# Attention in a hybrid gMLP / MLA decoder layer: probabilities as the stationary operand, next head's q, k, v between key steps

## The chip, the cores and the metric

One Trainium2 chip, all 8 cores. Each core computes one of the 8 sequences of the batch on its own; no data passes between cores. The metric is the device time in microseconds (us) of the slowest core.

TensorE is called PE in the profile (PEld is its weight load), VectorE DVE, ScalarE ACT, GpSimd POOL, SyncE SP. A matmul takes a stationary operand (at most 128x128, loaded into the array first) and a moving operand (up to 512 columns) and writes to a bank of PSUM. There are eight banks, each 128 partitions by 512 float32.

## The reference, cut to what matters

One decoder layer: a token-mixing sub-layer with two branches (gMLP spatial gating, and latent attention), then a gated MLP with a causal depthwise convolution. The change touches attention alone:

```python
q = (rmsnorm(q_lat, q_norm_g) @ w_uq).reshape(B, S, 16, 128 + 64)
kv = (rmsnorm(kv_lat, kv_norm_g) @ w_ukv).reshape(B, S, 16, 128 + 128)
q_nope, q_pe = q[..., :128], q[..., 128:]
k_nope, v = kv[..., :128], kv[..., 128:]
q_pe = apply_rope(q_pe, cos, sin)          # per head
k_pe = apply_rope(k_pe, cos, sin)          # one, shared by all heads
s = (q_nope @ k_nope^T + q_pe @ k_pe^T) * 192 ** -0.5      # S = 2048, causal
p = softmax(s, axis=-1)
o = p @ v                                  # (B, S, 16 heads * 128)
```

The output o of all heads goes through `w_branch_b`, is gated and added to the other branch.

## The kernel before, in words

The program of a core is written as a list of operations per engine. A helper (`P.op`, `P.dma`) notes what each operation reads and writes and puts waits on semaphores in front of it, by itself. Each engine runs its list in order. PSUM banks are tracked whole, and two engines that read one bank are kept apart. Most operations go through small helpers, so their line in the profile is that of the helper: `mm` (L338, a chain of matmuls), `act` (L345), `tt` (L349, tensor_tensor), `copy` (L363, CAST in the profile), `recip` (L366), a weight load (L217), `ada` (L400), transposes (L436).

The 2048 positions are worked in two blocks of 1024 (`blk` 0 and 1). A block goes through: norm and transpose of x, the gMLP projections and mixing, `branch` "a", `latents` (compressed q and kv, the rotary key), `attention`, `branch` "b", `wout_phase`, `ffn_up`, `ffn_down`. Queries of block 1 attend to keys of both blocks, so that block has more key steps.

Weights come through `WPool` in three slots, in a planned order, by casting DMAs issued on POOL. `next()` takes the next entry of the plan and issues loads up to `len(slots) - live` entries ahead, the current one counted. A load waits until the last readers of its slot, as far as they are written down at that point, are done. Attention uses one `pair` entry of 768 KB for two heads. In block 0, four `ada` entries of 2 MB (a part of the conditioning projection, 64 matmuls with one moving column) stand among them.

`attention` (L668) runs over 8 pairs of heads. For a pair it first computes, from `qgT` (512 x 1024) and `kvgT` (256 x 2048), all of q, k and v:

- for each half of 512 queries (`t`): the plain q of both heads (4 matmuls each, evicted by a DVE copy, L692), then the two rotary products of both heads together (4 + 4 matmuls), two DVE multiplies with cos and sin, and two DVE additions of 64 partitions each (L695 to L701). The other 64 partitions of each `Qr` are zero.
- for each head and each 512 keys: k by 2 matmuls and a DVE copy (L702 to L706).
- for each 256 keys: v of both heads by 4 matmuls of 256 columns (L713) and one ACT copy for each head (L718).

All these take their banks from `pbank`, which goes round seven of the eight, 1 to 7. Then come the two heads of the pair, one after the other (L719). For each `t` it goes over key blocks of 128 (`kb`), up to the diagonal. A step is: scores with keys stationary and queries moving (L749 plain, L750 rotary, and on the diagonal L752, which adds a mask), so that a tile holds 128 keys by up to 512 queries; the exponential by ACT into one of four `ptile`; and, two steps later, two matmuls with the exponentials moving: L759 with V stationary, which gives the output transposed (128 channels by 512 queries), and L760 with a matrix of ones stationary, which gives the sum of the exponentials in every partition. On diagonal steps the columns shrink from 512 to 384, 256, 128. At the end of a `t`, `finalize` takes the reciprocal of 128x512 and multiplies (L726, L727) into `oT`. The score banks rotate over 5 to 7; the outputs and sums stand in banks 2 and 3, or 1 and 4. At the end of each head the two pending steps are emitted before anything of the next head.

A head in block 0 has 4 + 8 = 12 steps, in block 1 12 + 16 = 28.

Of the kernel before, what the change touches and what calls it, by code (L numbers as in the profile page):

```python
# [234 lines left out]
def build():  # L235
# [34 lines left out]
    xtr = sb("xtr", [128, 10240], BF16)  # L270
# [22 lines left out]
    Qr = [scr[:, 2048:3072], scr[:, 3072:4096]]  # L293
    ptile = [scr[:, 8192 + 512 * k:8192 + 512 * (k + 1)] for k in range(4)]
    rec = scr[:, 10240:11264].bitcast(F32)
    rt1 = scr[:, 11264:12288].bitcast(F32)
    qgT = xtr[:, 0:4096].rearrange("p (c t) -> p c t", c=4)
    cos2 = xtr[:, 4096:5120]
    sin_s = xtr[:, 5120:6144]
    KV = ((scr[:, 4096:6144], scr[:, 6144:8192].rearrange("p (k d) -> p k d", k=16)),  # L300
          (xtr[:, 6144:8192], xtr[:, 8192:10240].rearrange("p (k d) -> p k d", k=16)))
# [27 lines left out]
    def pbank():  # L329
        b = 1 + prot["n"] % 7  # L330
        prot["n"] += 1
        return ps[b][:, :]
# [335 lines left out]
    def attention(plan, blk):  # L668
        T0 = blk * NT
        nk512 = (T0 + NT) // 512  # L670
        for pr in range(8):
            if plan:
                wp.declare(("pair", blk, pr), w_pair_d[pr].rearrange("p (k o) -> p k o", k=1), 1, 3072)
                if blk == 0 and pr % 2 == 1:
                    ada(True, 16 + pr // 2)
                continue
            rot["lo"], rot["cnt"] = 5, 3
            if pr == 0:
                P.op("pool", lambda e: e.memset(Qr[0][64:128, :], 0.0), writes=[Qr[0]])
                P.op("pool", lambda e: e.memset(Qr[1][0:64, :], 0.0), writes=[Qr[1]])  # L680
            w = wp.next(("pair", blk, pr))[:, 0, :]
            qn = w[:, 0:1024].rearrange("p (k o) -> p k o", k=4)
            qr = w[:, 1024:1536].rearrange("p (k o) -> p k o", k=4)
            qs = w[:, 1536:2048].rearrange("p (k o) -> p k o", k=4)
            kn = w[:, 2048:2560].rearrange("p (k o) -> p k o", k=2)
            vv = w[:, 2560:3072].rearrange("p (k o) -> p k o", k=2)
            for t in range(2):
                tsl = slice(t * 512, (t + 1) * 512)
                q = qgT[:, :, tsl]
                for hd in range(2):  # L690
                    out = pbank()
                    mm(out, [(qn[:, c, hd * 128:(hd + 1) * 128], q[:, c, :]) for c in range(4)], [qn, q])  # L692
                    copy(QnT[hd][:, tsl], out)
                pr_, psw = pbank(), pbank()
                for out, wsel in ((pr_, qr), (psw, qs)):  # L695
                    mm(out, [(wsel[:, c, :], q[:, c, :]) for c in range(4)], [wsel, q])
                tt(rt1, pr_, cos2[:, tsl], ALU.mult)
                tt(rec, psw, sin_s[:, tsl], ALU.mult)
                for hd in range(2):
                    p0 = 64 * hd  # L700
                    tt(Qr[hd][p0:p0 + 64, tsl], rt1[p0:p0 + 64, :], rec[p0:p0 + 64, :], ALU.add)  # L701
            for hd in range(2):  # L702
                for kt in range(nk512):
                    out, kv = pbank(), kvgT[:, :, kt * 512:(kt + 1) * 512]
                    mm(out, [(kn[:, c, hd * 128:(hd + 1) * 128], kv[:, c, :]) for c in range(2)], [kn, kv])
                    copy(KV[hd][0][:, kt * 512:(kt + 1) * 512], out)  # L706
            for kb0 in range(0, 4 * nk512, 2):
                out, kv = pbank(), kvgT[:, :, kb0 * 128:(kb0 + 2) * 128]

                def mmv(e, out=out, kv=kv, vv=vv):  # L710
                    for i in range(2):
# [4 lines left out]
                P.op("pe", mmv, reads=[vv, kv], writes=[out])  # L716
                for hd in range(2):
                    act(KV[hd][1][:, kb0:kb0 + 2, :], out.rearrange("p (i h d) -> p i h d", i=2, h=2)[:, :, hd, :], AF.Copy)  # L718
            for hd in range(2):  # L719
                h = 2 * pr + hd  # L720
                Kh, Vh = KV[hd]
                pend = []
                cnt = 0

                def finalize(t, po, psm):
                    recip(rec, psm)  # L726
                    tt(oT[:, h, t * 512:(t + 1) * 512], po, rec, ALU.mult)  # L727

                def emit_pend(ent):
                    f, rds, po, psm, fin = ent  # L730
                    P.op("pe", f, reads=rds, writes=[po, psm])
                    if fin is not None:
                        finalize(fin, po, psm)

                for t in range(2):
                    qa = (T0 + 512 * t) // 128
                    nkb = qa + 4
                    po, psm = (ps[2][:, :], ps[3][:, :]) if t == 0 else (ps[1][:, :], ps[4][:, :])
                    for kb in range(nkb):
                        i = kb - qa  # L740
                        c0 = 128 * i if i > 0 else 0
                        qsl = slice(t * 512 + c0, (t + 1) * 512)
                        out = gbank()
                        pt = ptile[cnt % 4][:, c0:512]
                        cnt += 1
                        ks = slice(kb * 128, (kb + 1) * 128)

                        def mms(e, out=out, i=i, c0=c0, qsl=qsl, ks=ks, hd=hd, Kh=Kh):
                            e.matmul(out[:, c0:512], lhsT=Kh[:, ks], rhs=QnT[hd][:, qsl], start=True, stop=False)  # L749
                            ins = e.matmul(out[:, c0:512], lhsT=kpe_dup[:, ks], rhs=Qr[hd][:, qsl], start=False, stop=(i < 0))  # L750
                            if i >= 0:
                                ins = e.matmul(out[:, c0:c0 + 128], lhsT=ident[:, :], rhs=maskneg[:, :], start=False, stop=True)  # L752
                            return ins
                        P.op("pe", mms, reads=[Kh[:, ks], kpe_dup[:, ks], QnT[hd][:, qsl], Qr[hd][:, qsl], ident[:, :], maskneg[:, :]],
                             writes=[out])
                        act(pt, out[:, c0:512], AF.Exp, scale=SCALE)

                        def mmo(e, kb=kb, c0=c0, pt=pt, nkb=nkb, po=po, psm=psm, Vh=Vh):
                            e.matmul(po[:, c0:512], lhsT=Vh[:, kb, :], rhs=pt, start=(kb == 0), stop=(kb == nkb - 1))  # L759
                            return e.matmul(psm[:, c0:512], lhsT=ones[:, :], rhs=pt, start=(kb == 0), stop=(kb == nkb - 1))  # L760
                        pend.append((mmo, [Vh[:, kb, :], pt, ones[:, :]], po, psm, t if kb == nkb - 1 else None))
                        if len(pend) > 2:
                            emit_pend(pend.pop(0))
                for ent in pend:
                    emit_pend(ent)
            if blk == 0 and pr % 2 == 1:
                ada(False, 16 + pr // 2)
            rot["lo"], rot["cnt"] = 4, 4

    def sumsq(bank, c):  # L770
        act(bank, bank, AF.Square, accum_out=stat[:, c:c + 1])
# [236 lines left out]
```

How the kernel before makes its waits and increments, by code:

```python
        def run(e, lst):  # L167
            for waits, fn, inc in lst:
                for s, v in waits:
                    e.wait_ge(semobj[s], v)
                if fn is None:
                    continue
                ins = fn(e)
                if inc is not None:
                    ins.then_inc(semobj[inc[0]], inc[1])
```

## Time and profile before

| | us |
|---|---|
| median of 3 runs | 5176.35 |
| lowest, highest | 4950.4, 5376.13 |
| the profiled execution, its own time | 4950.76 |
| its span, first to last instruction, slowest core (core 4) | 4949.0 |
| spans of the 8 cores | 4927.9 to 4949.0 |
| PE busy, mean granted clock on core 4 | 4377.7 (88%), 0.957 |

The span is what the rows are read from; the profiled execution's own time is 1.8 us longer. "Busy" counts a matmul from its start to the end of its passage through the array. Matmuls overlap in this, so the rate of a stream is read from the distance between starts and not from the duration. A granted clock of 1 is 2.4 GHz, a half is 1.2 GHz.

### The profile page before, as it was taken

To read this page: it belongs to the slowest core of one execution; us is meant where nothing else is said; L and a number is where in the kernel's file an instruction comes from. 1 tells how busy PE (TensorE), PEld (TensorE's weight loads), DVE (VectorE), ACT (ScalarE), POOL (GpSimd) and SP (SyncE) were. 2 spreads that over 40 slices of the span, in tenths; PEclk is the share of its full clock that TensorE was granted. 3 is DMA by queue.
4 is the path that set the end of the run, shared out by engine and by line. 5 is a ranking of instruction groups with operands and counts; after the bars stand their busy time and mean duration, and the time that the engine had idled before them with its cause. 6 is when DMAs were issued, how large, how long until landed. Compare 5 with 4: busy or idle time off the path is not lost.

```text
span 4949.0 us, 59571 instructions; the slowest of 8 cores (4927.9 to 4949.0 us)
## 1 busy us (share of the span) xinstructions
PE 4377.7 (88%) x22392; PEld 2056.5 (42%) x22392; DVE 1743.0 (35%) x2672; ACT 1476.6 (30%) x2775; POOL 200.9 (4%) x197
## 2 busy tenths in 40 slices
PE   0579998899979999999287999999999899999994
PEld 0334444444434444444143444444444344444442
DVE  0222007752155555400314114443422455555002
ACT  0331013420154444300133103555501444444000
POOL 1000000000000000000000000000000000000000
PEclk9989999999989999999688999999999999999997
DMA  9738872357874545445652542001234555453544
GB/s 153 134 52 109 107 119 43 54 93 104 116 178 72 82 70 84 64 73 87 194 108 42 84 69 43 14 7 24 45 73 79 149 94 86 69 85 58 83 74 148
DMA packets 330441, 423.56 MB, mean 86 GB/s; under 512 B 8496, under 2 KB 315696, under 8 KB 319408
## 3 DMA queue, kind: packets, MB, share of 16 engines
q0 software_dynamic: 312352, 328.22, 43.8%
q1 hardware_dynamic: 17808, 91.54, 5.6%
q8 instruction: 183, 3.00, 0.3%
q14 instruction: 98, 0.80, 0.1%
HBM read 714.37 MB, written 33.57 MB: 151 GB/s over the span
## 4 chain that ended last, share of the span: by engine, by line
PE 78%; DMA 8%; DVE 7%; ACT 3%; issue 3%; another core or an unknown queue 0%; DVEq 0%; SPq 0%; POOL 0%; ACTq 0%; POOLq 0%
PE ps L338 56%; PE ps L887 12%; PE ps L759 2%; DMA wslot<-w_ada 2%; PE ps L760 2%; DMA sb_big<-out 2%; PE ps L749 2%; PE ps L750 2%; ACT sb_scr L345 2%; DVE sb_scr L366 2%; DMA wslot<-w_ag 1%; DVE sb_scr L359 1%; DMA wslot<-w_out 1%; DMA wslot<-w_in 1%; DVE sb_big L359 1%
## 5 line engine op out<-in xcount | busy, mean ns | idle before, releaser
L345 ACT ACTIVATE sb_scr<-ps 128x512 f32<-128x512 f32 (+4 forms) x1304 | 709.4, 551 | 2145.2 <-PE ps L338 1534.2
L338 PE MATMUL ps<-sb_big,wslot 128*128 128x512 bf16 x5632 | 1239.3, 383 | 25.6 <-DMA wslot<-w_ag 9.2
L338 PE MATMUL ps<-sb_mrg,wslot 128*128 128x512 bf16 x5632 | 1219.0, 380 | 0.0
L338 PEld LDWEIGHTS ps<-sb_big,wslot 128*128 128x128 bf16 x5632 | 554.1, 99 | 700.8 <-issue 52.4
L338 PEld LDWEIGHTS ps<-sb_mrg,wslot 128*128 128x128 bf16 x5632 | 551.9, 98 | 666.3 <-issue 4.0
L359 DVE SCALAR_TENSOR_TENSOR sb_scr<-sb_scr,sb_cols 128x512 f32<-128x512 f32 x704 | 528.8, 751 | 541.7 <-ACT sb_scr L345 505.1
L887 PE MATMUL ps<-wslot,sb_big 128*128 128x512 bf16 x2048 | 452.5, 379 | 0.0
L366 DVE RECIPROCAL sb_scr<-ps 128x512 f32<-128x512 f32 x64 | 214.9, 3357 | 322.4 <-PE ps L760 321.5
L345 ACT ACTIVATE ps<-ps 128x512 f32<-128x512 f32 x128 | 74.5, 582 | 809.9 <-DVE sb_big L349 387.8
L349 DVE TENSOR_TENSOR sb_mrg<-ps,sb_scr 128x512 bf16<-128x512 f32 (+1 forms) x96 | 66.4, 691 | 689.2 <-PE ps L338 413.7
L887 PEld LDWEIGHTS ps<-wslot,sb_big 128*128 128x128 bf16 x2048 | 200.4, 98 | 241.6
L345 ACT ACTIVATE sb_scr<-ps,sb_cols 128x512 f32<-128x512 f32 x352 | 271.8, 772 | 0.0
L338 PE MATMUL ps<-wslot,sb_mrg 128*128 128x512 bf16 x1024 | 237.2, 395 | 5.7 <-DMA wslot<-w_out 5.7
L349 DVE TENSOR_TENSOR sb_scr<-ps,sb_scr 128x512 f32<-128x512 f32 x80 | 55.3, 691 | 498.1 <-PE ps L338 357.3
L338 PE MATMUL ps<-wslot,sb_big 128*128 128x512 bf16 x1024 | 223.7, 382 | 0.0
L436 PE MATMUL ps<-sb_ident,sb_scr 128*128 128x128 bf16 x512 | 52.2, 283 | 193.7 <-DVE sb_scr L354 92.8
L750 PE MATMUL ps<-sb_scr,sb_kpe_dup 128*128 128x512 bf16 (+3 forms) x640 | 222.7, 348 | 0.0
L760 PE MATMUL ps<-sb_scr,sb_ones 128*128 128x512 bf16 (+3 forms) x640 | 220.6, 347 | 0.0
L345 ACT ACTIVATE sb_scr<-sb_scr 128x512 bf16<-128x512 f32 (+1 forms) x208 | 171.8, 826 | 74.2 <-DVE sb_scr L359 46.3
L338 PE MATMUL ps<-sb_xtr,wslot 128*128 128x512 bf16 x512 | 130.8, 416 | 38.7 <-DVE sb_big L349 20.7
L400 PE MATMUL ps<-sb_scb,wslot 128*128 128x1 bf16 x1536 | 42.6, 164 | 133.5 <-DMA wslot<-w_ada 133.5
L338 PEld LDWEIGHTS ps<-wslot,sb_mrg 128*128 128x128 bf16 x1024 | 103.3, 102 | 133.9 <-issue 24.5
(112 smaller groups left out, 2973.5 us busy)
## 6 DMA issues: line engine op xcount, KB each, us to landing
wslot<-w_up POOLq DMA_DIRECT2D x44, 2048.0 KB, 14.7
wslot<-w_ada POOLq DMA_DIRECT2D x24, 2048.0 KB, 28.3
wslot<-w_down POOLq DMA_DIRECT2D x32, 1408.0 KB, 10.7
sb_scr<-x SPq DMA_DIRECT2D x32, 1024.0 KB, 6.4
wslot<-w_in POOLq DMA_DIRECT2D x16, 2048.0 KB, 17.1
wslot<-w_ag POOLq DMA_DIRECT2D x16, 2048.0 KB, 14.7
wslot<-w_bg POOLq DMA_DIRECT2D x16, 2048.0 KB, 14.9
wslot<-w_out POOLq DMA_DIRECT2D x8, 2048.0 KB, 15.5
```

The costliest lines, as they stand in the source:

```text
L338: ins = e.matmul(out, lhsT=a, rhs=b, start=(k == 0), stop=(k == len(pairs) - 1))
L345: P.op("act", lambda e: e.activation(out=out, in_=in_, func=func, **kw), reads=[in_] + extra + list(reads), writes=[out] + acc + list(writes))
L349: P.op(eng, lambda e: e.tensor_tensor(out=out, in0=in0, in1=in1, op=op), reads=[in0, in1], writes=[out])
L359: P.op("dve", lambda e: e.scalar_tensor_tensor(out=out, in0=in0, scalar=s, in1=in1, op0=op0, op1=op1), reads=[in0, in1] + extra, writes=[out])
L366: P.op("dve", lambda e: e.reciprocal(out=out, in_=in_), reads=[in_], writes=[out])
L400: ins = e.matmul(out[:, oc:oc + 1], lhsT=wv[:, kc, oc * 128:(oc + 1) * 128], rhs=scb[:, kc:kc + 1], start=(kc == 0), stop=(kc == KC - 1))
L436: ins = e.transpose(out=pv[:, k * 128:(k + 1) * 128], in_=src[:, kc * 128:(kc + 1) * 128], identity=ident[:, :])
L749: e.matmul(out[:, c0:512], lhsT=Kh[:, ks], rhs=QnT[hd][:, qsl], start=True, stop=False)
L750: ins = e.matmul(out[:, c0:512], lhsT=kpe_dup[:, ks], rhs=Qr[hd][:, qsl], start=False, stop=(i < 0))
L759: e.matmul(po[:, c0:512], lhsT=Vh[:, kb, :], rhs=pt, start=(kb == 0), stop=(kb == nkb - 1))
L760: return e.matmul(psm[:, c0:512], lhsT=ones[:, :], rhs=pt, start=(kb == 0), stop=(kb == nkb - 1))
L887: ins = e.matmul(out, lhsT=g[k], rhs=wv[:, k, :], start=(q == 0 and k == 0), stop=(q == 3 and k == 10))
```

## The change

Only `attention` and the tiles it uses change.

- The exponentials of a step become the stationary operand, 128 keys by 128 queries at a time, and V the moving one. V has a 129th column of ones, so that column 128 of the result is the sum. A step has one to four such matmuls of 129 columns. The output stands with queries in the partitions, four quarters in two banks. L760 is gone.
- At the end of a `t`, per bank: a reciprocal of two columns and a multiply into `on` (bf16). Three steps later four transposes (`turn_o`) bring it back to channels by queries, and a DVE copy writes `oT`.
- q, k and v are computed per head by `gen(h)`, as a list of tasks. The tasks of head h + 1 are dealt out evenly between the key steps of head h. Head 0's stand alone ahead of the loop. Rotary q is still made for two heads at once, in the list of the even head, and `Qr` is double now. The sine product is written back to its PSUM bank. v comes per head, 8 matmuls of 128 columns and one ACT copy for 512 keys.
- The pending attends go on across heads; nothing drains between them.
- Banks: 0 to 3 hold outputs, in two pairs that alternate. All else (scores, tasks, transposes, `ada`) rotates over 4 to 7.
- `wp.live` is 2 in attention, so loads are issued one entry less ahead. `ada` entries stand at other places of the plan.

The diff, cut to its core:

```diff
+    Qr = [[oT[:, 14, :], oT[:, 15, :]], [scr[:, 2048:3072], scr[:, 3072:4096]]]
+    on = scr[:, 10256:10768].rearrange("p (s d) -> p s d", s=4)
+    KV = ((scr[:, 4096:6144], scr[:, 6144:8208].rearrange("p (k d) -> p k d", k=16)),
+          (xtr[:, 6144:8192], xtr[:, 8192:10256].rearrange("p (k d) -> p k d", k=16)))
...
+                if blk == 0 and (pr in (2, 4, 6) or pr == 7):
+                    ada(True, 16 + (pr - 1) // 2)
+            return
+        for i in range(2):
+            for z in (Qr[0][i], Qr[1][i]):
+                half = z[64:128, :] if i == 0 else z[0:64, :]
+                P.op("pool", lambda e, half=half: e.memset(half, 0.0), writes=[z])
+            one = KV[i][1][:, :, 128:129]
+            P.op("pool", lambda e, one=one: e.memset(one, 1.0), writes=[one, Qr[0][0], Qr[0][1], Qr[1][0], Qr[1][1]])
...
+            def rope(t):
+                pr_, psw = gbank(), gbank()
...
+                tt(rt1, pr_, cos2[:, tsl], ALU.mult)
+                tt(psw, psw, sin_s[:, tsl], ALU.mult)
+                for i in range(2):
+                    p0 = 64 * i
+                    tt(Qr[pr % 2][i][p0:p0 + 64, tsl], rt1[p0:p0 + 64, :], psw[p0:p0 + 64, :], ALU.add)
...
+                    for i in range(4):
                         for c in range(2):
-                            ins = e.matmul(out[:, i * 256:(i + 1) * 256], lhsT=kv[:, c, i * 128:(i + 1) * 128], rhs=vv[:, c, :],
+                            ins = e.matmul(out[:, i * 128:(i + 1) * 128], lhsT=kv[:, c, i * 128:(i + 1) * 128], rhs=vv[:, c, dsl],
                                            start=(c == 0), stop=(c == 1))
...
+                act(Vh[:, 4 * kt:4 * kt + 4, 0:128], out.rearrange("p (i d) -> p i d", i=4), AF.Copy)
+
+            work = [lambda t=t: nope(t) for t in range(2)]
+            if hd == 0:
+                work += [lambda t=t: rope(t) for t in range(2)]
+            for kt in range(nk512):
+                work += [lambda kt=kt: keys(kt), lambda kt=kt: values(kt)]
+            return work
...
-                            e.matmul(po[:, c0:512], lhsT=Vh[:, kb, :], rhs=pt, start=(kb == 0), stop=(kb == nkb - 1))
-                            return e.matmul(psm[:, c0:512], lhsT=ones[:, :], rhs=pt, start=(kb == 0), stop=(kb == nkb - 1))
+        def attend(h, t, kb, nkb, pt, s0, po):
+            v = KV[h % 2][1][:, kb, :]
+            def go(e):
+                for s in range(s0, 4):
+                    ins = e.matmul(po[s // 2][:, s % 2 * 256:s % 2 * 256 + 129], lhsT=pt[:, s * 128:(s + 1) * 128], rhs=v,
+                                   start=(kb == 0 and s % 2 == 0), stop=(kb == nkb - 4 + s), skip_group_check=True)
+                return ins
+            P.op("pe", go, reads=[pt[:, s0 * 128:512], v], writes=po)
+            if kb == nkb - 1:
+                for b in range(2):
+                    o3 = po[b].rearrange("p (s c) -> p s c", s=2)
+                    rs = stat[:, 48 + 2 * b:50 + 2 * b]
+                    recip(rs.unsqueeze(2), o3[:, :, 128:129])
+                    tt(on[:, 2 * b:2 * b + 2, :], o3[:, :, 0:128], rs.unsqueeze(2).broadcast_to([128, 2, 128]), ALU.mult)
+                late.append([3, lambda: turn_o(h, t)])
...
+        wp.live = 2
+        for w in gen(0):
+            w()
+        for h in range(16):
+            nxt = gen(h + 1) if h < 15 else []
+            steps = sum((T0 + 512 * t) // 128 + 4 for t in range(2))
+            done, total = 0, len(nxt)
+            for t in range(2):
...
+                for kb in range(nkb):
+                    pt, s0 = scores(h, t, kb, qa, k)
+                    k += 1
+                    pend.append((h, t, kb, nkb, pt, s0, po))
+                    if len(pend) > 2:
+                        attend(*pend.pop(0))
+                    step()
+                    done += 1
+                    while nxt and len(nxt) > (steps - 2 - done) * total / steps:
+                        nxt.pop(0)()
...
+            if blk == 0 and h % 4 == 3:
+                ada(False, 16 + h // 4)
+        wp.live = 1
+        while pend:
+            attend(*pend.pop(0))
+        while late:
+            late.pop(0)[1]()
```

`gbank` takes the next bank of the rotation (4 to 7 outside the old `attention`). `step` counts the entries of `late` down once per key step and runs those that reach zero.

## Rows read from the trace of the kernel before

**Rows 1.** The page, engine totals and costliest groups, whole span.

```profile
PE 4377.7 (88%) x22392; PEld 2056.5 (42%) x22392; DVE 1743.0 (35%) x2672; ACT 1476.6 (30%) x2775; POOL 200.9 (4%) x197
...
L366 DVE RECIPROCAL sb_scr<-ps 128x512 f32<-128x512 f32 x64 | 214.9, 3357 | 322.4 <-PE ps L760 321.5
...
L760 PE MATMUL ps<-sb_scr,sb_ones 128*128 128x512 bf16 (+3 forms) x640 | 220.6, 347 | 0.0
```

**Rows 2.** Both attention stages: length; busy PE, PEld, DVE, ACT, POOL (instructions); clock; DMA.

```profile
791.19:1066.96 275.77, 239.66 (x1537) 124.75 (x1536) 210.47 (x195) 110.54 (x257) 10.16 (x12) 0.96 0.41 68
...
3061.22:3586.90 525.68, 490.02 (x2561) 233.37 (x2559) 229.19 (x224) 281.34 (x577) 6.64 (x9) 0.98 0.13 24
```

**Rows 3.** Timeline of PE, full steps in block 1: start, duration.

```profile
3093.70 0.38 PE L749 MATMUL ps<-sb_scr 128*128 128x512 bf16 x1
...
3098.45 0.22 PE L752 MATMUL ps<-sb_maskneg,sb_ident 128*128 128x128 bf16 x1
```

**Rows 4.** Timelines, pauses of PE at pair starts, first exponentials, stage ends.

```profile
860.38 8.74 PE L338 MATMUL ps<-sb_xtr,wslot 128*128 128x512 bf16 x28 [2.06 <-DVE sb_modc L349]
...
1070.79 9.39 PE L338 MATMUL ps<-sb_big,wslot 128*128 128x512 bf16 x36 [2.08 <-DVE sb_scr L366]
...
3080.52 0.38 PE L759 MATMUL ps<-sb_scr 128*128 128x512 bf16 x1 [0.89 <-ACT sb_scr L345]
...
3124.13 1.89 PE L338 MATMUL ps<-sb_xtr,wslot 128*128 128x512 bf16 x8
3128.75 6.93 PE L338 MATMUL ps<-sb_xtr,wslot 128*128 128x512 bf16 x24 [2.73 <-DVE sb_big L349]
...
3139.62 0.59 PE L338 MATMUL ps<-sb_kvgT,wslot 128*128 128x512 bf16 x2 [0.92 <-DVE sb_scr L363]
3140.22 4.62 PE L713 MATMUL ps<-wslot,sb_kvgT 128*128 128x256 bf16 x32
...
3590.65 9.59 PE L338 MATMUL ps<-sb_big,wslot 128*128 128x512 bf16 x31 [3.68 <-DVE sb_scr L366]
```

**Rows 5.** Timelines, short matmuls with a weight load each, and the loads.

```profile
806.04 0.22 PE L749 MATMUL ps<-sb_scr 128*128 128x128 bf16 x1
806.10 0.22 PE L750 MATMUL ps<-sb_scr,sb_kpe_dup 128*128 128x128 bf16 x1
...
806.21 0.33 PE L759 MATMUL ps<-sb_scr 128*128 128x384 bf16 x1
...
1066.96 1.74 PE L400 MATMUL ps<-sb_scb,wslot 128*128 128x1 bf16 x64
...
1392.60 1.06 PE L436 MATMUL ps<-sb_ident,sb_scr 128*128 128x128 bf16 x16
1393.49 0.81 PE L338 MATMUL ps<-wslot,sb_mrg 128*128 128x512 bf16 x3
...
L760 PEld LDWEIGHTS ps<-sb_scr,sb_ones 128*128 128x128 bf16 x192 | 18.8, 98 | 6.4
```

**Rows 6.** Groups of DVE in block 0's stage (busy us, mean ns), and a timeline row.

```profile
L366 DVE RECIPROCAL sb_scr<-ps 128x512 f32<-128x512 f32 x32 | 107.4, 3357 | 45.0 <-PE ps L760 44.2
...
L349 DVE TENSOR_TENSOR sb_scr<-sb_scr 64x512 bf16<-64x512 f32 x32 | 22.0, 687 | 2.2 <-DVE sb_scr L349 0.2
...
1071.35 0.15 DVE L349 TENSOR_TENSOR sb_modc<-ps,sb_cols 128x4 f32<-128x4 f32 x1
```

**Rows 7.** ACT: exponentials in block 1, and a stage's table loads (one each stage).

```profile
3079.78 1.57 ACT L345 ACTIVATE sb_scr<-ps 128x512 bf16<-128x512 f32 x3
...
L345 ACT ACT_TABLE_LOAD x1 | 1.3, 1283 | 0.0
```

**Rows 8.** Weight loads around block 0's attention (780 to 1200 us).

```profile
wslot<-w_ada POOLq DMA_DIRECT2D x7, 2048.0 KB, 17.3
wslot<-w_bg POOLq DMA_DIRECT2D x6, 2048.0 KB, 16.0
...
874.18 0.54 POOL L217 DMA_DIRECT2D wslot<-w_pair  x1 [15.04 <-PE ps L713]
```

More of the change, by code:

```diff
@@ L269, in build @@
     scr = sb("scr", [128, 12288], BF16)
-    xtr = sb("xtr", [128, 10240], BF16)
+    xtr = sb("xtr", [128, 10272], BF16)
     kvgT = sb("kvgT", [128, 2, S], BF16)
@@ L292, in build @@
     QnT = [scr[:, 0:1024], scr[:, 1024:2048]]
[L293 to L296, printed above, removed]
+    Qr = [[oT[:, 14, :], oT[:, 15, :]], [scr[:, 2048:3072], scr[:, 3072:4096]]]
+    ptile = [scr[:, 8208 + 512 * k:8208 + 512 * (k + 1)] for k in range(4)]
+    on = scr[:, 10256:10768].rearrange("p (s d) -> p s d", s=4)
+    rt1 = scr[:, 10768:11792].bitcast(F32)
     qgT = xtr[:, 0:4096].rearrange("p (c t) -> p c t", c=4)
@@ L670, in attention @@
         nk512 = (T0 + NT) // 512
-        for pr in range(8):
-            if plan:
+        if plan:
+            for pr in range(8):
                 wp.declare(("pair", blk, pr), w_pair_d[pr].rearrange("p (k o) -> p k o", k=1), 1, 3072)
[L674 to L687, printed above, removed]
+                if blk == 0 and (pr in (2, 4, 6) or pr == 7):
+                    ada(True, 16 + (pr - 1) // 2)
+            return
@@ new lines, in attention, with weights @@
+        for i in range(2):
[4 more added lines that the diff above has]
+            P.op("pool", lambda e, one=one: e.memset(one, 1.0), writes=[one, Qr[0][0], Qr[0][1], Qr[1][0], Qr[1][1]])
+        wcur = {}
+        def weights(pr):
+            if pr not in wcur:
+                w = wp.next(("pair", blk, pr))[:, 0, :]
+                wcur[pr] = [w[:, a:b].rearrange("p (k o) -> p k o", k=k) for a, b, k in
+                            ((0, 1024, 4), (1024, 1536, 4), (1536, 2048, 4), (2048, 2560, 2), (2560, 3072, 2))]
+            return wcur[pr]
@@ L688, in attention, with gen, nope @@
+        def gen(h):
+            pr, hd = h // 2, h % 2
+            Kh, Vh = KV[hd]
+            dsl = slice(hd * 128, (hd + 1) * 128)
+            def nope(t):
+                qn = weights(pr)[0]
+                out, q = gbank(), qgT[:, :, t * 512:(t + 1) * 512]
+                mm(out, [(qn[:, c, dsl], q[:, c, :]) for c in range(4)], [qn, q])
+                copy(QnT[hd][:, t * 512:(t + 1) * 512], out)
+            def rope(t):
                 tsl = slice(t * 512, (t + 1) * 512)
                 q = qgT[:, :, tsl]
[L690 to L693, printed above, removed]
@@ L694, in attention @@
-                pr_, psw = pbank(), pbank()
-                for out, wsel in ((pr_, qr), (psw, qs)):
-                    mm(out, [(wsel[:, c, :], q[:, c, :]) for c in range(4)], [wsel, q])
-                tt(rt1, pr_, cos2[:, tsl], ALU.mult)
[L698 to L711, printed above, removed]
+                pr_, psw = gbank(), gbank()
+                for out, w in ((pr_, weights(pr)[1]), (psw, weights(pr)[2])):
+                    mm(out, [(w[:, c, :], q[:, c, :]) for c in range(4)], [w, q])
+                tt(rt1, pr_, cos2[:, tsl], ALU.mult)
+                tt(psw, psw, sin_s[:, tsl], ALU.mult)
@@ new lines, in rope, with keys, values @@
+                for i in range(2):
+                    p0 = 64 * i
+                    tt(Qr[pr % 2][i][p0:p0 + 64, tsl], rt1[p0:p0 + 64, :], psw[p0:p0 + 64, :], ALU.add)
+            def keys(kt):
+                kn = weights(pr)[3]
+                out, kv = gbank(), kvgT[:, :, kt * 512:(kt + 1) * 512]
+                mm(out, [(kn[:, c, dsl], kv[:, c, :]) for c in range(2)], [kn, kv])
+                copy(Kh[:, kt * 512:(kt + 1) * 512], out)
+            def values(kt):
+                vv = weights(pr)[4]
+                out, kv = gbank(), kvgT[:, :, kt * 512:(kt + 1) * 512]
+                def go(e):
+                    for i in range(4):
@@ L712, in mmv @@
                         for c in range(2):
-                            ins = e.matmul(out[:, i * 256:(i + 1) * 256], lhsT=kv[:, c, i * 128:(i + 1) * 128], rhs=vv[:, c, :],
+                            ins = e.matmul(out[:, i * 128:(i + 1) * 128], lhsT=kv[:, c, i * 128:(i + 1) * 128], rhs=vv[:, c, dsl],
                                            start=(c == 0), stop=(c == 1))
                     return ins
-                P.op("pe", mmv, reads=[vv, kv], writes=[out])
-                for hd in range(2):
-                    act(KV[hd][1][:, kb0:kb0 + 2, :], out.rearrange("p (i h d) -> p i h d", i=2, h=2)[:, :, hd, :], AF.Copy)
@@ L719, in attention @@
[L719 to L758, printed above, removed]
-                            e.matmul(po[:, c0:512], lhsT=Vh[:, kb, :], rhs=pt, start=(kb == 0), stop=(kb == nkb - 1))
-                            return e.matmul(psm[:, c0:512], lhsT=ones[:, :], rhs=pt, start=(kb == 0), stop=(kb == nkb - 1))
[L761 to L765, printed above, removed]
@@ L766, in attention @@
-            if blk == 0 and pr % 2 == 1:
-                ada(False, 16 + pr // 2)
-            rot["lo"], rot["cnt"] = 4, 4
+                P.op("pe", go, reads=[vv, kv], writes=[out])
+                act(Vh[:, 4 * kt:4 * kt + 4, 0:128], out.rearrange("p (i d) -> p i d", i=4), AF.Copy)
[4 more added lines that the diff above has]
+                work += [lambda kt=kt: keys(kt), lambda kt=kt: values(kt)]
@@ new lines, in gen, with scores, go @@
+            return work
+        pend, late = [], []
+        ocnt = [0]
+        def scores(h, t, kb, qa, k):
+            hd = h % 2
+            i = kb - qa
+            c0 = 128 * i if i > 0 else 0
+            qsl = slice(t * 512 + c0, (t + 1) * 512)
+            out, pt = gbank(), ptile[k % 4]
+            ks = slice(kb * 128, (kb + 1) * 128)
+            Kh, Qh, Rh = KV[hd][0][:, ks], QnT[hd][:, qsl], Qr[h // 2 % 2][hd][:, qsl]
+            kp = kpe_dup[:, ks]
+            def go(e):
+                e.matmul(out[:, c0:512], lhsT=Kh, rhs=Qh, start=True, stop=False)
+                ins = e.matmul(out[:, c0:512], lhsT=kp, rhs=Rh, start=False, stop=(i < 0))
+                if i >= 0:
+                    ins = e.matmul(out[:, c0:c0 + 128], lhsT=ident[:, :], rhs=maskneg[:, :], start=False, stop=True)
+                return ins
+            P.op("pe", go, reads=[Kh, kp, Qh, Rh, ident[:, :], maskneg[:, :]], writes=[out])
+            act(pt[:, c0:512], out[:, c0:512], AF.Exp, scale=SCALE)
+            return pt, max(i, 0)
@@ new lines, in turn_o, with go, step @@
+        def turn_o(h, t):
+            out = gbank().bitcast(BF16)[:, 0:512]
+            def go(e):
+                for s in range(4):
+                    ins = e.transpose(out=out[:, s * 128:(s + 1) * 128], in_=on[:, s, :], identity=ident[:, :])
+                return ins
+            P.op("pe", go, reads=[on[:, :, :], ident[:, :]], writes=[out])
+            copy(oT[:, h, t * 512:(t + 1) * 512], out)
+        def step():
+            for ent in late:
+                ent[0] -= 1
+            while late and late[0][0] <= 0:
+                late.pop(0)[1]()
@@ new lines, in attention @@
+        wp.live = 2
+        for w in gen(0):
+            w()
+        k = 0
+        for h in range(16):
[3 more added lines that the diff above has]
+            for t in range(2):
+                qa = (T0 + 512 * t) // 128
+                nkb = qa + 4
+                po = [ps[2 * (ocnt[0] % 2)][:, :], ps[2 * (ocnt[0] % 2) + 1][:, :]]
+                ocnt[0] += 1
+                for kb in range(nkb):
[8 more added lines that the diff above has]
+                        nxt.pop(0)()
+            while nxt:
+                nxt.pop(0)()
+            if blk == 0 and h % 4 == 3:
+                ada(False, 16 + h // 4)
@@ L770, in sumsq @@
+        wp.live = 1
+        while pend:
+            attend(*pend.pop(0))
+        while late:
+            late.pop(0)[1]()
     def sumsq(bank, c):
```

4 lines of the change are left out of this document (2 added, 2 removed).

## The prediction

> **What bounds the kernel now.** I read four views in this order. First the engine totals of the page [rows 1]: TensorE is busy 88% of the span, DVE and ACT a third of it. So a change pays only where it takes columns or idle time from TensorE. Two groups of the page touch this change: the ones-matmul of L760 (640 of them) and the RECIPROCAL of L366, 3.36 us each.
>
> Second, the two attention stages as windows [rows 2]: 275.8 us in block 0 (first q matmul to last L760) and 525.7 us in block 1. I compare each with what its matmuls need back to back. In a run of full steps 22 matmuls of 512 columns start in 4.75 us, 215.7 ns each, that is 512 columns at 2.4 GHz plus 2.3 ns [rows 3]; I use this pair, columns/2.4 ns + 2.3 ns, for every matmul. Block 0 issues 507,904 columns in 1344 matmuls plus three `ada` calls of 1.6 us: 211.6 + 3.1 + 4.8 = 219.5 us. Block 1 issues 1,097,728 columns in 2560: 457.4 + 5.9 = 463.3 us. Left over: 56.3 and 62.4 us. To these I add the pauses after the last L760 of each stage, 2.1 and 3.7 us [rows 4]. Gaps are 124.5 us in all.
>
> Third, where these gaps are [rows 4]. At a pair's start TensorE stops 2.73 us after eight matmuls: a bank handed to the new pair's q still holds the sums of the old head, and DVE reads them for 3.36 us. There are casts to wait for at 0.92 us, the first exponentials at 0.89 us, and in block 1 the 32 value matmuls take 4.62 us where 32 of 109 ns would take 3.5: two ACT copies per bank pace them. After some pauses the clock stands at its lower level: 28 matmuls take 8.74 us behind `ada` and a 2.06 us pause, where 6.0 is normal (nearly all the excess is 15 matmuls near 0.4 us apart, the 1.2 GHz level). The same costs some 2.5 us on other pair starts.
>
> **The change, part by part.**
>
> *Ones-matmul out, probabilities stationary.* Per head and block the old kernel moved 4608 (block 0) or 12,800 (block 1) columns through L759 and as many through L760. Now every 128-query quarter is a matmul of 129 columns: 10 + 26 = 36 in block 0, 42 + 58 = 100 in block 1, or 4644 and 12,900 columns. Turning adds 8 matmuls of 128 columns a head. Q, k and score columns stay; value matmuls become twice as many at half the width. So per head block 0 now has 12,288 (q, k, v) + 10,240 (scores, mask) + 4644 + 1024 = 28,196 columns in 112 matmuls: 12.0 us; sixteen heads and three `ada`: 196.9 us. Block 1: 16,384 + 26,624 + 12,900 + 1024 = 56,932 in 236: 24.3 us; sixteen heads: 388.2 us. Against 219.5 and 463.3 this saves 22.6 + 75.1 = 97.7 us.
>
> The doubtful price is that of a short matmul with a new weight load each: 2176 of L759's successor, 256 transposes, 768 value matmuls, 3200 in all. No row shows 129 columns. Rows 5 show 128: from 806.04 three score matmuls of 128 columns with a load each, and the L759 behind them, start 0.17 us over all, 55 ns apart, and sixteen transposes start over 0.89 us, 55.6 ns each, with sixteen loads. The lower end is 53.8 ns (129 columns at 2.4 GHz), the upper 154 ns, if the 98 ns that a load shows ran in series. I take 56: the transposes are the same shape, and 64 loads go through in 1.74 us, so loads alone can come every 27 ns.
>
> The Trainium skill speaks against this part: "TensorE: Matmul & The Clock Gate", section "Back-to-back issue gap", puts a sustained stream of load and matmul pairs at about 81 ns for 128 columns. By that, as an estimate from that page, 3200 x 25 = 81 us would be lost and the time would be 4857 us. The sixteen-transpose row here disagrees, at 55.6 ns.
>
> *Normalising.* 64 reciprocals of 128x512 (3.36 us) leave DVE for reciprocals of two columns, half-width multiplies and a cast: by the 0.69 us of 128x512 and the 0.15 us of a 128x4 operation [rows 6], about 2 x (0.15 + 0.4) + 0.65 = 1.75 us a pass instead of 4.05. The new result waits three steps for its transposes, some 2 us, so TensorE should seldom wait.
>
> *Dealing out.* The gap at each pair's start goes: scores always have a next instruction, nothing drains between heads, and the output banks (0 to 3) are no longer handed to other work. Value evictions fall between exponentials. ACT then has per full step 0.5 us (three exponentials in 1.57 us with one latency of 0.6 inside [rows 7]) against 0.65 us of TensorE, plus 0.5 us per four value blocks: about 14 us of 24.3 a head in block 1, 5.5 of 12 in block 0. It stays covered. Copy and Exp alternating costs no table load: a stage has one load [rows 7], though seven later pairs go from copies to exponentials. Were it not so, about 90 insertions at 2 x 1.28 us would be some 230 us of ACT; the count excludes it.
>
> What is late next is the rope work. It takes two of four banks, shared now with scores; DVE then needs two multiplies and two additions of 0.69 us each, 2.8 us [rows 6], the second bank until the last. TensorE comes round to that bank after three others. In block 1 tasks lie about two steps apart (28 steps, 12 tasks), so 1.95 to 2.3 us pass: 0.4 us stall per rope, 1.2 a pair with neighbours, 8 us. In block 0, eight tasks go in twelve steps and both rope tasks follow each other, so about 2 us a pair, 14 us. Bounds: nothing (the DVE queue is empty), and 2.8 us for each of 32 ropes, 90 us.
>
> *Remaining gaps.* The first head's q, k, v stand alone with four banks instead of seven and are DVE-paced, 2 us, then the first exponentials cost 1.5 us: 7 us for both blocks. Other heads 0.3 us each: 9. At the end two last attends, DVE and the transposes have no cover: 2 us, twice. Lower clock behind `ada`: 5. Sum 14 + 8 + 7 + 9 + 4 + 5 = 47; it replaces 124.5, so 77.5 us go.
>
> *Queues.* POOL issues weight loads one ahead less. But a load goes as soon as the last reader of its slot is done, since POOL waits for nothing else: the `pair` load at 874.18 was released by a matmul of the pair before [rows 8]. Counting slots through the new order, the one that receives an `ada` block is free at least two heads (24 us) ahead of its use, against 17.3 us to landing [rows 8]; the first `w_bg` block of 16.0 us likewise. Cost zero; without that cover, up to 16 us for each of four. The four half-tile memsets and the ones columns are some 4 us on idle POOL ahead of the first rope: hidden behind the last latents.
>
> **Sum.** 97.7 + 77.5 = 175 us. The profiled execution took 4950.8 us (span 4949.0 plus 1.8). 4950.8 - 175 = **4776 us**. The median of the runs shown is 5176.4; the profiled run agrees with the lowest of them (4950.4), and I forecast from there.
>
> **Rivals.**
>
> A. *Loads exposed at each instruction boundary.* Weights are now fresh from ACT, and a load can't go ahead of the semaphore that releases it. 640 steps x 98 ns = 63 us: 4839. For: the stationary operand is new in each step, where V and ones were old. Against: at 806.21 an L759, which has a wait in front of it in the program, starts on the 55 ns beat [rows 5]. The Trainium skill's 81 ns named above would be the same trouble spread over all short matmuls, at 4857 us; no chance is set aside for it beyond this rival's.
>
> B. *Bank waits replace the drains.* Four banks serve scores, q, k, v, ropes and transposes. 288 dealt tasks at 0.3 us, half of the 0.60 to 0.92 us cast waits of today: 86 us, of which 22 us are in my sum, plus slow clock behind some: with ropes at their upper bound 4850 to 4900, middle 4862. For: DVE has 210 of 276 us in block 0 now [rows 2]. Against: the reciprocals alone are 107 us of that [rows 6].
>
> C. *Loads in series (slower).* Place: the four matmuls of each attend. Price: 98 ns for each of 3200 short matmuls, 314 us: 5090. It decides as soon as a short matmul costs 55 ns more than its columns (3200 x 55 = 175), a spacing of 111 ns. Against: both chains of rows 5.
>
> D. *Nearly no gaps:* floor 585 us plus 7: about 4735.
>
> **How the numbers follow.** Forecast (4740 to 4815) 0.68; A 0.10; B 0.12; C 0.04; D 0.06. Leaving out C and the upper half of B, the range is 4735 to 4850. A measurement of this kernel tells about 2% from no change, a boundary of 4852 us. Faster: 0.68 + 0.10 + 0.06 + a quarter of B = 0.87. Within 2%: the rest of B, 0.09. Slower: C, 0.04.
>
> **What would show it.** Right: L759's successor starts about 56 ns apart in runs of four; the stages take about 225 and 408 us; RECIPROCAL has only small forms in attention; no pause of TensorE over 2 us at pair boundaries; DVE below 75% in block 0; weight loads cause no wait. Wrong: spacing above 80 ns (A or C), or many TensorE waits on DVE and ACT with banks as their cause (B), or waits for w_ada or w_bg. A stage as long as before would mean that the idle time only changed its place.

## The result and the profile after

The changed kernel took 4865.5 us at its fastest and 4869.1 us in the median; over the kernel before, on the same chips, the ratio is 0.983 (interval 0.981 to 0.986). It is 1.7% faster: the interval leaves no doubt about the sign, but the gain is less than the 2% that the prediction had named as the boundary of no change. The forecast was 3.5%, 4776 us, with a range that ended at 4850. So the sign was right and the size was off by half. In some executions the cores of one die show a lower granted clock than the others and take longer (5018.9 us here), so fastest times are compared with fastest times, and where no execution was free of it, the cores of the other die.

First the two attention stages as windows (columns as in [rows 2], DVE third and ACT fourth of the engines):

```profile
785.10:1041.96 256.86, 217.39 (x2050) 134.83 (x2049) 134.53 (x293) 107.80 (x225) 11.27 (x13) 0.98 0.44 71
3035.02:3509.90 474.88, 416.75 (x3649) 247.89 (x3648) 157.78 (x321) 277.50 (x513) 6.62 (x9) 1.00 0.16 28
```

Measured alike, from the first q matmul to the first matmul of the next stage, before had 279.6 and 529.4 us, 809.0 in all. Here it is 731.7. So 22.7 + 54.6 = 77.3 us of the 84.4 us between the two spans (4949.0 and 4864.6) were won here. The forecast for both windows together was 809.0 - 175.2 = 633.8 us (the stages at about 225 and 408). They took 98 us more, so all of the missing time is in attention, and some two thirds of it in block 1. The time outside the two windows differs by up to 20 us between executions, with the same instructions in it (4124 us on core 0 of this kernel, 4144 on core 0 of the first experiment's), which is why I compare stages below where I can. A window's ends are good to 0.2 us, as a matmul record can be missing.

Where TensorE stands there is told by its waits. The view is PE's idle time before the instructions of one line, by what ended it (us, times); first the transposes of the changed kernel (L787), then its attends (L770), as successors of L759 and L760 in [rows 1]:

```profile
L787 PE MATMUL ps<-sb_ident,sb_scr x256: 216/217/314, 805.3 to 3509.8; 128*128 128x128 bf16 x128
its engine sat idle before it (us, times) until:
  ACT sb_scr L345: 43.5, 60
  DVE sb_scr L349: 3.7, 3
  DVE ps L349: 0.8, 1
...
L770 PE MATMUL ps<-sb_xtr,sb_scr x1088: 217/220/315, 813.0 to 3507.9; 128*128 128x129 bf16 x182
...
  ACT sb_scr L345: 30.6, 103
```

The first group makes no sense by the source. A transpose reads `on`, which DVE writes, and it waited for DVE only four times. 60 times of 64 it waited for ACT, which writes nothing that it reads. PE's timeline in block 1 shows one such place. The ACT row under it is the instruction that was waited for:

```profile
3121.60 0.38 PE L757 MATMUL ps<-sb_scr,sb_kpe_dup 128*128 128x512 bf16 x1
3121.82 0.39 PE L770 MATMUL ps<-sb_scr 128*128 128x129 bf16 x4
3123.03 0.38 PE L787 MATMUL ps<-sb_ident,sb_scr 128*128 128x128 bf16 x4 [0.82 <-ACT sb_scr L345]
```

```profile
3122.19 0.60 ACT L345 ACTIVATE sb_scr<-ps 128x512 bf16<-128x512 f32 x1 [0.91 <-PE ps L757]
```

And DVE's timeline, the last multiply that writes `on`:

```profile
3120.88 0.42 DVE L349 TENSOR_TENSOR sb_scr<-ps,sb_stat 128x256 bf16<-128x256 f32 x1
```

The transposes stand until the exponential of the step's own scores is through: it ends at 3122.79, they start at 3123.03. `on` had been ready since 3121.30. The price of a short matmul is seen where nothing waits. Four of 129 columns, each with its own load, and the score behind them:

```profile
3131.80 0.39 PE L770 MATMUL ps<-sb_scr 128*128 128x129 bf16 x4
3132.03 0.27 PE L756 MATMUL ps<-sb_scr 128*128 128x256 bf16 x1
```

The score starts 0.22 to 0.23 us behind the first of the four in such steps, some 56 ns each. Nor is a load exposed in front of them: at 3121.82 the first starts 0.22 us behind the score before it (3121.60), the distance of two full matmuls in a row.

**Where such a wait can come from.** Waits are put in by the tracker (`Prog.where`), which notes what is read and written in granules; for tiles with long rows, as `scr`, a granule is 64 bytes (L80). V with 129 columns made the tiles behind it start 16 elements, 32 bytes, later. Before, `ptile` began at byte 16384 = 256 x 64. Now it begins at 16416 = 256.5 x 64, and each `ptile` shares a granule with its neighbour; `on` begins at 20512 = 320.5 x 64 and shares one with `ptile[3]`, and one with `rt1` behind it. By the tracker, then, an exponential into `ptile[3]` writes a piece of `on`, and the exponential into `ptile[k+1]` writes a piece of `ptile[k]`. I call this false sharing. All passes have 4, 8, 12 or 16 steps, so a transpose emitted three steps behind the last attend always follows an exponential into `ptile[3]`. The rival is what my prediction had (rival B): four banks in rotation, for transposes, scores and tasks.

### The profile page after: what moved, and what is told of

The parts are those of the page before. It is cut to its first block, busy times and chain, and to the rows that moved or that the text cites. A ratio compares the mean times of both kernels' runs of the same rounds, so it can differ in the third digit from the quotient of the medians.

```text
span 4864.6 us, 62719 instructions; the slowest of 8 cores (4847.9 to 4864.6 us)
## 1 busy us (share of the span) xinstructions
PE 4270.9 (88%) x23928; PEld 2076.4 (43%) x23928; DVE 1590.0 (33%) x2864; ACT 1470.4 (30%) x2679; POOL 204.9 (4%) x205
## 4 chain that ended last, share of the span: by engine, by line
PE 77%; DMA 9%; ACT 5%; DVE 5%; issue 3%; ACTq 0%; DVEq 0%; POOL 0%; SPq 0%; POOLq 0%
PE ps L338 57%; PE ps L948 12%; ACT sb_scr L345 4%; DMA wslot<-w_ada 3%; DMA sb_big<-out 2%; PE ps L770 2%; PE ps L756 2%; PE ps L757 2%; DMA wslot<-w_out 1%; DMA wslot<-w_ag 1%; DVE sb_scr L359 1%; DVE sb_big L359 1%; DMA sb_scr<-x 1%; PE ps L729 1%; DMA wslot<-w_in 1%
## 5 line engine op out<-in xcount | busy, mean ns | idle before, releaser
L345 ACT ACTIVATE sb_scr<-ps 128x512 bf16<-128x512 f32 (+2 forms) x1256 | 700.2, 565 | 2070.0 <-PE ps L338 1535.8
L338 PE MATMUL ps<-sb_big,wslot 128*128 128x512 bf16 x5632 | 1234.5, 382 | 17.7 <-DMA wslot<-w_ag 13.9
L338 PE MATMUL ps<-sb_mrg,wslot 128*128 128x512 bf16 x5632 | 1218.4, 380 | 0.0
L338 PEld LDWEIGHTS ps<-sb_big,wslot 128*128 128x128 bf16 x5632 | 553.3, 98 | 688.8 <-issue 37.5
L338 PEld LDWEIGHTS ps<-sb_mrg,wslot 128*128 128x128 bf16 x5632 | 551.7, 98 | 665.9 <-issue 3.3
L948 PEld LDWEIGHTS ps<-wslot,sb_big 128*128 128x128 bf16 x2048 | 200.4, 98 | 241.6
L349 DVE TENSOR_TENSOR sb_mrg<-ps,sb_scr 128x512 bf16<-128x512 f32 (+1 forms) x96 | 66.4, 691 | 692.1 <-PE ps L338 416.9
L338 PE MATMUL ps<-wslot,sb_mrg 128*128 128x512 bf16 x1024 | 234.9, 392 | 4.1 <-DMA wslot<-w_out 4.1
L338 PE MATMUL ps<-wslot,sb_big 128*128 128x512 bf16 x1024 | 223.0, 381 | 0.0
L349 DVE TENSOR_TENSOR sb_scr<-ps,sb_scr 128x512 f32<-128x512 f32 x80 | 55.3, 692 | 496.8 <-PE ps L338 355.9
L338 PEld LDWEIGHTS ps<-wslot,sb_mrg 128*128 128x128 bf16 x1024 | 102.4, 101 | 130.8 <-issue 20.1
L948 PE MATMUL ps<-wslot,sb_xtr 128*128 128x512 bf16 x640 | 157.7, 379 | 0.0
L338 PEld LDWEIGHTS ps<-wslot,sb_big 128*128 128x128 bf16 x1024 | 100.6, 98 | 121.6 <-issue 2.2
L363 DVE CAST sb_scr<-ps 128x512 bf16<-128x512 f32 x112 | 77.1, 691 | 190.5 <-PE ps L338 190.2
L436 PEld LDWEIGHTS ps<-sb_ident,sb_scr 128*128 128x128 bf16 x512 | 45.3, 129 | 210.6 <-issue 210.3
## 6 DMA issues: line engine op xcount, KB each, us to landing
wslot<-w_out POOLq DMA_DIRECT2D x8, 2048.0 KB, 14.5
```

What stands on the lines that cost most here:

```text
L338: ins = e.matmul(out, lhsT=a, rhs=b, start=(k == 0), stop=(k == len(pairs) - 1))
L345: P.op("act", lambda e: e.activation(out=out, in_=in_, func=func, **kw), reads=[in_] + extra + list(reads), writes=[out] + acc + list(writes))
L349: P.op(eng, lambda e: e.tensor_tensor(out=out, in0=in0, in1=in1, op=op), reads=[in0, in1], writes=[out])
L363: P.op(eng, lambda e: e.tensor_copy(out=out, in_=in_), reads=[in_], writes=[out])
L436: ins = e.transpose(out=pv[:, k * 128:(k + 1) * 128], in_=src[:, kc * 128:(kc + 1) * 128], identity=ident[:, :])
L948: ins = e.matmul(out, lhsT=g[k], rhs=wv[:, k, :], start=(q == 0 and k == 0), stop=(q == 3 and k == 10))
```

## The experiments

**Tiles aligned.** Three tiles move by 32 bytes:

```diff
-    ptile = [scr[:, 8208 + 512 * k:8208 + 512 * (k + 1)] for k in range(4)]
-    on = scr[:, 10256:10768].rearrange("p (s d) -> p s d", s=4)
-    rt1 = scr[:, 10768:11792].bitcast(F32)
+    ptile = [scr[:, 8224 + 512 * k:8224 + 512 * (k + 1)] for k in range(4)]
+    on = scr[:, 10272:10784].rearrange("p (s d) -> p s d", s=4)
+    rt1 = scr[:, 10784:11808].bitcast(F32)
```

> The changed kernel with ptile, on and rt1 each moved up by 16 elements (32 bytes) in scr, so that each starts on a multiple of 64 bytes; nothing else. The tracker notes reads and writes in granules of 64 bytes, and in the changed kernel neighbours share one. Theory (false sharing): the waits of the transposes (L787, 43.5 us) and of the attends (L770, 30.6 us) for ACT all but vanish, both attention stages together get 70 to 100 us shorter, the time is 4770 to 4800. Rival (four banks: a transpose or attend waits for the bank or for its own exponential): no instruction moves, waits stay, 4860 to 4870.

Measured: 4788.5 us at its fastest, 4793.7 in the median, ratio to before 0.966 (0.962 to 0.969). The same two views of this kernel, windows and the waits of L787 and L770:

```profile
800.04:1033.26 233.22, 208.27 (x2017) 135.17 (x2049) 133.02 (x293) 106.49 (x225) 11.27 (x13) 0.99 0.47 76
3022.32:3438.89 416.57, 394.60 (x3584) 256.79 (x3648) 157.03 (x321) 275.31 (x513) 6.62 (x9) 1.00 0.18 32
```

```profile
  DVE sb_scr L349: 9.8, 20
...
  ACT sb_scr L345: 0.3, 1
```

The waits for ACT are gone: 43.5 to none, 30.6 to 0.3 us. The stages take 649.8 us instead of 731.7, 82 us less, with the same instructions in the same order. The transposes now wait for DVE 20 times, a wait that stood behind the false one. The banks were not it. (The kernel before, run beside the first four experiments, took 4956.1 us at its fastest, beside the last four 4954.0, against 4949.4 beside the changed kernel; times of different experiments compare to within that.)

**Only `on` freed.** `on` and `rt1` move as above, `ptile` stays.

> The changed kernel with only on and rt1 moved up by 16 elements; the four ptile still share granules with each other. False sharing: the waits of L787 for ACT go (43.5 us and some 0.17 us for each of 60), those of L770 stay near 30 us; about 4815. Rival (banks): no change from 4866.

Measured: 4829.8 us at its fastest, stages 241.3 and 453.9 us. The transposes wait for ACT no more; the attends as before:

```profile
  ACT sb_scr L345: 31.6, 105
```

So the two sharings are two costs, taken in this order: 731.7 - 695.2 = 36.5 us for the transposes, 695.2 - 649.8 = 45.4 us for the attends. (`rt1` moved too, so its sharing with `on` is in the first of them.) I had expected 51 for the first. Most of the difference is in other waits that the false ones had covered: those of scores and tasks for rotary work of DVE (L756, L338 and L729 for L349) are 25.0 us here and 17.5 in the changed kernel, those of the transposes for DVE 6.7 and 3.7. The second cost is more than the 31.6 us of the list. The list counts a matmul busy to the end of its passage, and a full one lasts 0.38 us where the next starts after 0.22, so each of the 105 waits is short by 0.16: 31.6 + 17 = some 49 us.

**Transposes four steps behind.**

```diff
-                late.append([3, lambda: turn_o(h, t)])
+                late.append([4, lambda: turn_o(h, t)])
```

> The changed kernel with the transposes four key steps after the last attend instead of three. All passes have 4, 8, 12 or 16 steps, so by false sharing each transpose stands right behind the exponential into ptile[3] with 3, and one step behind it with 4: its wait per transpose falls from 0.73 us to 0.1 to 0.3 us, L787's sum from 43.5 to under 15 us, the time by some 30 us. By banks the transpose still takes the next bank of the rotation, and the wait stays near 0.7 us each.

Measured on cores 0 to 3: their median span is 4838.9 us, 14.5 less than that of the changed kernel's cores 0 to 3 (4853.4). The span hides half of the gain. On core 0 the two stages take 244.3 + 459.1 = 703.4 us against 731.7, 28.3 less, close to the 30 expected, and the rest of the program took 13.6 us more in this execution. On each of the four cores the transposes waited for DVE's `on` twice, 3.2 us, and never for ACT. So the wait hangs on which `ptile` was written last, and not on the bank: the transposes still take the next bank of the rotation. The gain is less than the 43.5 us of the list because other waits grew: those of the attends for ACT from 30.9 to 39.2 us (104 to 135 times, core 2), those for rotary work from 17.5 to 24.6 us.

**The kernel before, with its `ptile` shifted.** The same fault put into the old kernel, with `scr` made 32 elements larger.

```diff
-    ptile = [scr[:, 8192 + 512 * k:8192 + 512 * (k + 1)] for k in range(4)]
-    rec = scr[:, 10240:11264].bitcast(F32)
-    rt1 = scr[:, 11264:12288].bitcast(F32)
+    ptile = [scr[:, 8208 + 512 * k:8208 + 512 * (k + 1)] for k in range(4)]
+    rec = scr[:, 10272:11296].bitcast(F32)
+    rt1 = scr[:, 11296:12320].bitcast(F32)
```

> The kernel before with its four ptile moved up by 16 elements (scr 32 elements larger, rec and rt1 behind them on multiples of 64 bytes), so that neighbouring ptile share a granule and nothing else changes. False sharing: an L759 now waits for the exponential of the next step too, which ends some 0.98 us after its scores while only 0.86 us of other work lies between: 0.1 to 0.2 us at each of 640 steps, 60 to 130 us slower, 5010 to 5080. Rival (the alignment of a tile is of no account): 4950.

Measured: ratio to before 1.009 (1.0045 to 1.013), 44 us slower, the sign expected with a smaller size. The stages take 288.7 and 568.1 us, 47.8 more than before. L759 waited for ACT 7.4 us in 19 cases before, and now:

```profile
  ACT sb_scr L345: 33.5, 61
```

I had laid 0.1 to 0.2 us on each of 640 steps. 47.8/640 is 0.07. Two things make it less. Only three of four steps can pay, as `ptile[3]` shares with nothing here. And in a stretch of full steps PE's timeline shows that only every second one waits:

```profile
3136.28 0.38 PE L750 MATMUL ps<-sb_scr,sb_kpe_dup 128*128 128x512 bf16 x1
3136.69 0.38 PE L759 MATMUL ps<-sb_scr,sb_xtr 128*128 128x512 bf16 x1
```

L759 starts 0.41 us behind the matmul before it, 0.2 late, and again so at 3138.61, while the one between, at 3137.55, starts on time: the step that waited has given it the time it needed. The list shows nothing of such waits, as they are barely longer than the 0.16 us of passage. The same sharing of `ptile` costs 45 us in the changed kernel, whose step is 0.65 us against 0.86 and whose attend takes half as long; why it isn't more there wasn't worked out.

**The tracker's granule.** Tiles stay where the change put them; only the tracker's arithmetic is finer.

```diff
-        g = 4 if row <= 4096 else 64
+        g = 4 if row <= 4096 else 32
```

> The changed kernel with every tile where the change put it, and the tracker noting large tiles in granules of 32 bytes instead of 64 (all the moved tiles start on multiples of 32). Only semaphore waits can differ. False sharing in the tracker: the same as with aligned tiles, 4785 to 4800, no L787 or L770 wait for ACT. Rival (the hardware reads or writes tiles slower that don't start on 64 bytes, and the aligned kernel gained by that): 4866.

Measured: 4788.6 us at its fastest, against 4788.5 with aligned tiles. The stages:

```profile
794.75:1029.08 234.33, 212.57 (x2050) 136.13 (x2049) 133.17 (x293) 106.68 (x225) 11.27 (x13) 0.98 0.49 75
3016.00:3432.56 416.56, 398.07 (x3649) 256.77 (x3648) 157.08 (x321) 275.28 (x513) 6.61 (x9) 1.00 0.18 31
```

416.56 against 416.57 us in block 1. In block 0 it is 1.1 us more, at a granted clock of 0.98 against 0.99. The addresses are those of the slow kernel, and the 82 us are gone all the same, so the hardware had no part in them. The cause is the waits alone.

**No dealing.** The aligned kernel, with the tasks of the next head in one lump behind a head's steps:

```diff
-                    while nxt and len(nxt) > (steps - 2 - done) * total / steps:
-                        nxt.pop(0)()
```

> The aligned kernel without dealing: all tasks of head h + 1 are emitted in one lump behind head h's steps; pending attends still go across. My sum put the removal of the pair-start gaps at 77 us without telling dealing from the rest. Theory 1 (the gaps went because nothing drains and the long reciprocals and shared output banks are gone; dealing only hides some DVE pacing of ropes and casts): 1 to 2 us a head, 4815 to 4845. Theory 2 (dealing itself hides the q, k, v work's waits): most of the 77 us comes back, 4860 to 4880.

Measured: 4832.2 us at its fastest, ratio to before 0.974 (0.972 to 0.977), stages 253.8 and 436.4 us; the transposes wait for DVE 57 times, 18.3 us. The time is that of theory 1: dealing is worth 40.4 us of the stages (690.2 - 649.8), 1.3 us a head. But theory 1 held dealing for the smaller part, and 40.4 us are two thirds of the 61.5 us by which the gaps shrank from before to the aligned kernel (124.5 to 63). The clock shows a part of it: 0.94 of full in block 0 here, 0.99 with dealing.

**The sine product in SBUF.** On the aligned kernel, with a new tile `rt2` behind `rt1` (`scr` 544 elements larger):

```diff
-                tt(psw, psw, sin_s[:, tsl], ALU.mult)
+                tt(rt2, psw, sin_s[:, tsl], ALU.mult)
...
-                    tt(Qr[pr % 2][i][p0:p0 + 64, tsl], rt1[p0:p0 + 64, :], psw[p0:p0 + 64, :], ALU.add)
+                    tt(Qr[pr % 2][i][p0:p0 + 64, tsl], rt1[p0:p0 + 64, :], rt2[p0:p0 + 64, :], ALU.add)
```

> The aligned kernel with the sine product written to SBUF (a tile rt2, scr 544 elements larger) instead of back into its bank, so that the bank is free after the second multiply and not after both additions. If what is late next is this bank, the waits of L756 and L338 for rotary DVE work (27 us, 0.92 + 0.71 us a pair in block 1, 0.47 + 0.29 + 1.41 in block 0) fall to under 12 us and the time by 12 to 22 us. If DVE's queue is late and not the bank, they stay, with the time within 4 us of the aligned kernel.

This tests the one gap that I had worked out myself. In the aligned kernel the timeline of PE shows it in block 1 at each odd head, twice:

```profile
3065.70 0.38 PE L756 MATMUL ps<-sb_scr,sb_xtr 128*128 128x512 bf16 x1 [0.92 <-DVE sb_scr L349]
...
3070.71 0.38 PE L756 MATMUL ps<-sb_scr,sb_xtr 128*128 128x512 bf16 x1 [0.71 <-DVE sb_scr L349]
```

Measured: 4770.0 us at its fastest, ratio 0.961 (0.958 to 0.964), 18.5 us less than aligned. The stages are 229.1 and 402.9 us, 4.1 and 13.7 less. The time is in the range expected of a late bank. In block 1 the 14 waits of scores for rotary work, 11.4 us (some 13.6 with 0.16 for each), are gone: there it was the bank. In block 0 the waits of scores and tasks for DVE went only from 15.7 to 13.7 us, and half of them now end with a cast of DVE instead of an addition: so there, by these names, DVE's queue itself is late behind two rotary tasks in a row; no run tried the queue alone. Each theory holds in one block. (Block 0's 229.1 us end with a wait of 1.0 us for w_bg, which the aligned kernel hasn't.)

**Both, and the transposes four steps behind.** The kernel of the last run with 4 for 3 in `late.append`.

> The kernel of the run before this one with the transposes four steps behind instead of three. L787 waits 9.8 us for the normalised output, 20 times. They go but for the two at the stage ends (3.1 us): 5 to 8 us less than the run before this one, some 4765.

Measured: 4759.6 us at its fastest, 4763.5 in the median, ratio to before 0.960 (0.957 to 0.963). It is the fastest kernel here, 106 us below the changed one and 4% below the one before. Its stages:

```profile
794.87:1018.08 223.21, 206.40 (x2018) 135.29 (x2049) 132.52 (x295) 107.62 (x225) 11.29 (x13) 0.99 0.48 78
3003.18:3401.34 398.16, 390.33 (x3585) 257.11 (x3649) 156.89 (x321) 275.23 (x513) 6.63 (x9) 1.00 0.19 33
```

621.4 us, where the matmuls back to back need 196.9 + 1.6 + 388.2 = 586.7 (1.6 is the fourth `ada`, which falls into this window). It is 10.4 us below the run before, a little more than the 5 to 8 expected. The transposes still wait 6.1 us in 9 cases, and not only the two at the stage ends, 1.6 us each, where nothing covers them.

## Why the prediction was wrong

- **Columns saved, 97.7 us: right.** The short matmul costs the 56 ns that I took, not 81 or 154, and rivals A and C fall. (A head of block 1 has 228 matmuls and not the 236 that I counted, 0.3 us in all.) The Trainium skill's 81 ns for 128 columns ("TensorE: Matmul & The Clock Gate", "Back-to-back issue gap") holds neither for the sixteen transposes of [rows 5] nor for 2176 matmuls of this kind here.
- **Gaps: the step that failed.** I let 124.5 us of gaps become 47. They became 731.7 - 586.7 = 145 us, more than before the change. The sum says of the new transposes "TensorE should seldom wait" and of ACT "it stays covered". Both were worked out for waits that the source's data asks for: an attend for its own exponential, two steps old, and a transpose for `on`, three steps old. The diff's first lines moved tiles by 32 bytes, and I took this as bookkeeping. What the runs showed in its place: 36.5 us of transposes and 45.4 us of attends that wait for exponentials of other tiles, 82 us in all. Without them the kernel takes 4788 us, 12 above the forecast and inside the range; its stages are 159.2 us shorter than before, where the sum had 175.2.
- **The rest of the gap sum.** In the aligned kernel 649.8 - 586.7 = 63 us are left where I had 47. The rope work, which I priced at 1.2 us a pair in block 1 and 2 us in block 0, waits 0.92 + 0.71 and 0.47 + 0.29 + 1.41 us: the place is right, and so is the mechanism in block 1, where it costs a third more than I had; in block 0 the size is right by luck, as the experiment with `rt2` points to DVE's queue more than to the bank. Of the 20 transposes that wait 9.8 us for DVE my sum had only those at the stage ends.
- **Rival B** had a middle of 4862 us, within 4 us of the result, and was wrong: it blamed the banks. The number alone would have confirmed it. The finer granule, which changes no bank, refuted it.
- **Dealing.** Of the 77.5 us that I gave to vanished gaps the aligned kernel has 61.5. Taking the dealing out gives 40 of them back; the reciprocals of 3.36 us, the shared output banks and the drain together some 21, and how these divide wasn't tried.
- **Queues, table loads: right.** ACT has one table load of 1.3 us in each stage. Weight loads cost next to nothing in attention; only at the start of `branch` "b" in block 0 the faster kernels show a wait for w_bg, 1.0 and 0.56 us in the last two. DVE is busy 52% of block 0's stage, where I set 75% as the sign.

## What to carry to other kernels

When a wait in the profile names an engine that writes nothing the instruction reads, look at what the tracker believes, not at the engine: false sharing between neighbours in one tile looks just like a real dependency, and its place follows the buffer number. A change that shifts the start of a tile needs its granule checked with the same care as its instructions; here 32 bytes cost 82 us, half of what the change could bring. And a cheap way to tell a wait from the hardware's doing is to keep every address and make only the tracking finer.

## What was new of the hardware

Tiles that start on 32 but not on 64 bytes cost nothing that a run could show: block 1's stage took 416.56 us with such tiles and 416.57 with aligned ones. A moving operand with rows of 258 bytes ran at the same 56 ns for 129 columns as columns and issue alone would give (129/2.4 + 2.3). A DVE multiply of 128x512 that writes back to its PSUM bank takes about as long as one to SBUF: 690 against 691 ns in the changed kernel's block 0, 698 against 690 in block 1.
